# A 256-token, two-block network on one core: where the last weights, keys and first expert rows are loaded, and who turns retention's queries and keys

## The reference, cut to what matters

```python
def rotary(x, pos):
    cos, sin = jnp.cos(ang), jnp.sin(ang)
    x1, x2 = x[..., :half], x[..., half:]
    return jnp.concatenate([x1 * cos - x2 * sin, x1 * sin + x2 * cos], axis=-1)
# retention: q = rotary(q, pos); k = rotary(k, pos) * (RET_QK_DIM ** -0.5), 4 heads of 256

def one_block(xb):                                   # 256 tokens, 8 heads, 16 experts chosen per head
    qh = (xb @ wq).reshape(PEER_BLOCK, H_P, 2, D_QP // 2)
    s1 = jnp.einsum('thd,hnd->thn', qh[:, :, 0], sub_keys[0])
    s2 = jnp.einsum('thd,hnd->thn', qh[:, :, 1], sub_keys[1])
    v1, i1 = lax.top_k(s1, TOPK)
    v2, i2 = lax.top_k(s2, TOPK)
    cand = (v1[..., :, None] + v2[..., None, :]).reshape(PEER_BLOCK, H_P, TOPK * TOPK)
    sc, ci = lax.top_k(cand, TOPK)
    idx = ...                                        # i1 * 128 + i2 of the 16 best pairs
    gate_w = jax.nn.softmax(sc, axis=-1)
    act = jax.nn.gelu(jnp.einsum('thkd,td->thk', expert_u[idx], xb), approximate=False)
    return jnp.einsum('thk,thkd->td', gate_w * act, expert_v[idx])
```

## Time and profile before

| what | us |
|---|---|
| median of 3 runs | 1898.67 |
| lowest and highest | 1896.62, 1901.51 |
| the profiled execution, whole | 1897.0 |
| its span in the trace | 1895.7 |

### The profile page before, as it was taken

How to read it: one execution, slowest core, us unless ns; L and a number is a source line. 1 busy time by engine, 2 the same in 40 slices (tenths; PEclk the granted TensorE clock), 3 DMA queues, 4 the chain that set the end, 5 groups by cost and what they waited for, 6 DMA issues and landing times.

```text
span 1895.7 us, 23366 instructions
## 1 busy us (share of the span) xinstructions
PE 1712.7 (90%) x9248; PEld 1305.8 (69%) x9248; DVE 1201.8 (63%) x2123; ACT 748.2 (39%) x1314; POOL 414.2 (22%) x359
## 2 busy tenths in 40 slices
PE   7989999999999998989999999887888877787879
PEld 6869988977799888989989988873333333333333
DVE  5776654685566547864352665778667776667754
ACT  4555543434445435874353644442112212112211
POOL 0330000130000000003011000135454454454441
PEclk9999999999999999999999999999898898988889
DMA  6325555444455553422231323599999999999997
GB/s 246 111 102 185 194 180 196 164 158 169 149 178 187 181 189 140 164 108 91 88 112 47 110 89 125 183 422 378 422 421 421 422 421 421 422 420 422 421 422 295
DMA packets 62668, 453.87 MB, mean 239 GB/s; under 512 B 6968, under 2 KB 7096, under 8 KB 7904
## 3 DMA queue, kind: packets, MB, share of 16 engines
q0 software_dynamic: 36864, 268.45, 34.1%
q1 hardware_dynamic: 25040, 178.27, 26.2%
q10 hardware_dynamic: 656, 5.66, 0.8%
HBM read 451.15 MB, written 1.05 MB: 239 GB/s over the span
## 4 chain that ended last, share of the span: by engine, by line
PE 26%; DMA 17%; DVE 4%; ACT 2%; issue 1%; POOL 0%; DVEq 0%
DMA uv_rows<-expert_uv,index 16%; PE banks L2404 13%; PE banks L564 3%; PE banks L566 3%; PE banks L565 3%; DVE uv_rows L2551 2%; PE banks L2223 1%; PE banks L1894 0%; PE banks L1883 0%; POOL uv_rows L2574 0%; DMA sb_peer<-constants_peer 0%; DVE weights_lo L559 0%; PE banks L2370 0%; ACT diag L2455 0%; PE banks L1876 0%
## 5 line engine op out<-in xcount | busy, mean ns | idle before, releaser
L2404 PE MATMUL banks<-uv_rows,diag 128*128 128x512 f32 x1024 | 506.2, 658 | 123.3 <-ACT diag L2455 118.1
L559 DVE TENSOR_TENSOR weights_lo<-weights,weights_hi 128x1024 fp32r<-128x1024 f32 x336 | 419.0, 1288 | 262.5 <-ACT weights_hi L550 262.4
L2404 PEld LDWEIGHTS banks<-uv_rows,diag 128*128 128x128 f32 x1024 | 214.0, 212 | 414.9 <-issue 267.5
L550 ACT ACTIVATE weights_hi<-weights 128x1024 fp32r<-128x1024 f32 x336 | 336.9, 1052 | 373.9 <-PE banks L566 358.4
L564 PE MATMUL banks<-x_hi,weights_hi 128*128 128x256 f32 (+1 forms) x1472 | 428.6, 291 | 11.0 <-DVE weights_lo L559 5.5
L566 PE MATMUL banks<-x_hi,weights_lo 128*128 128x256 f32 (+1 forms) x1472 | 421.6, 286 | 0.0
L565 PE MATMUL banks<-x_lo,weights_hi 128*128 128x256 f32 (+1 forms) x1472 | 421.4, 286 | 0.0
L2551 DVE CUSTOM_DVE_ANT_0 uv_rows<-uv_rows,tokens 128x1024 f32<-128x1024 f32 x256 | 306.3, 1224 | 161.9 <-DMA uv_rows<-expert_uv,index 161.9
L2574 POOL DMA_INDIRECT uv_rows<-expert_uv,index x256 | 310.1, 1211 | 345.5 <-PE banks L2404 287.1
L564 PEld LDWEIGHTS banks<-x_hi,weights_hi 128*128 128x128 f32 x1472 | 283.3, 192 | 17.1 <-DVE weights_lo L559 7.4
L566 PEld LDWEIGHTS banks<-x_hi,weights_lo 128*128 128x128 f32 x1472 | 283.1, 192 | 0.0
(11 more groups left out here) (377 smaller groups left out, 2086.0 us busy)
## 6 DMA issues: line engine op xcount, KB each, us to landing
weights<-weights SPq DMA_DIRECT2D x168, 1024.0 KB, 4.8
uv_rows<-expert_uv,index POOLq DMA_INDIRECT x256, 18.4
sb_first<-constants_first ACTq DMA_DIRECT2D x1, 1920.0 KB, 8.8
sb_always<-constants_always ACTq DMA_DIRECT2D x1, 1627.5 KB, 7.0
sb_peer<-constants_peer ACTq DMA_DIRECT2D x1, 1544.0 KB, 8.0
h<-x SPq DMA_DIRECT2D x1, 1024.0 KB, 5.7
out<-h SPq DMA_DIRECT2D x4, 256.0 KB, 4.7
sb_now<-constants_now ACTq DMA_DIRECT2D x1, 216.0 KB, 4.7
```

Source lines behind the costliest of these rows:

```text
L550: self.act.activation(self.w_hi[b % SLOTS][:, f], self.raw[b % SLOTS][:, f], ACT.Copy).then_inc(self.hi_made, 1)
L559: self.dve.tensor_tensor(self.w_lo[b % SLOTS][:, f], self.raw[b % SLOTS][:, f], self.w_hi[b % SLOTS][:, f], ALU.subtract).then_inc(self.lo ...
L2404: mm = pe.matmul(self.bank(2 * t + half), self.diag[:, k, :], self.uv[n % NUV][:, f], start=(u < NT and k == 0), stop=(u >= UNITS - NT and ...
```

## The change

It has four parts.

1. **Blocks 164 to 167** (`AHEAD` = 4) are no longer loaded into the weight slots but into four of the early row buffers: 164 and 165 as soon as the mixer's last sum is made, 166 and 167 right behind block 163, all before block 164 is used. Gathers 5 and 6 now go to the weight slots, 7 to 10 to the four ahead buffers; each waits for the low part of blocks 162 to 167 in turn.
2. **The keys** are loaded by ACT at the first merge step instead of behind the mixer's last row product.
3. **Rows 0 to 3** (`FIRST_ROWS`) are dotted, gated and added between query blocks 6 and 7 instead of after all of them. The key scores use banks 0, 1, 2, 3, 0, 2, 3, 2 (`SCORE_BANK`), so that banks 0 and 1 are free. Gathers 13 to 16 take the buffers of rows 0 to 3, and only 17 to 19 wait for PE's reading of block 167. DVE computes the tokens one block earlier, the dots of rows 0 to 3 after block 4's split and those of rows 4 to 7 ahead of block 7, chooses unit 1 over blocks 5 and 6 instead of 4 to 6, and chooses unit 2 after the third group of unit 0 instead of the second.
4. **Retention**: DVE turns queries and keys, two heads at a time, in four calls of six instructions of 128 x 2 x 256. POOL turns nothing.

```diff
-        self.uv += [slots_of[j] for j in (0, 1, 2, 4, 3, 5)]
+        self.ahead = self.uv[EARLY - AHEAD:]
+        self.uv = self.uv[:EARLY - AHEAD] + slots_of[:SLOTS] + self.ahead + [slots_of[j] for j in (2, 4, 3, 5)]
...
     def sync_blocks(self):
-        w = self.ins["weights"]
-        for b in range(N_BLOCKS):
+        w, own = self.ins["weights"], N_BLOCKS - AHEAD
+        for b in range(own):
+            if b == own - 1:
+                self.sp.wait_ge(self.rows_done.sem, self.rows_done.at("mix_out", 4))
+                self.sync_ahead(own)
+                self.sync_ahead(own + 1)
             if b >= SLOTS:
                 self.sp.wait_ge(self.lo_made, PARTS * (b - SLOTS + 1))
             self.sp.dma_start(self.raw[b % SLOTS][:, :], w[b]).then_inc(self.block_full[b % SLOTS], 16)
+        self.sync_ahead(own + 2)
+        self.sync_ahead(own + 3)
...
-            if s >= 5:
-                self.vector_rotate(s - 5)
+            if s >= 4 and s < 7:
+                self.vector_rotate(*((0, 0), (0, 1), (1, 0))[s - 4])
...
-                self.vector_rotate(3)
+                self.vector_rotate(1, 1)
...
-        pool.wait_ge(self.turns_scaled, 2)
-        for hd in range(RET_H):
-            pool.wait_ge(*self.cols_freed("ret_qk", 4 + hd))
-            self.rotate(pool, self.g_step, hd, 8 + 2 * hd, self.ret_tmp[:, 2:4, :], self.ret_rot_k)
...
+            if s == 0:
+                act.dma_start(self.t_peer[:, :], self.ins["constants_peer"]).then_inc(self.peer_landed, 16)
...
+            if s == st.n - 2:
+                pe.wait_ge(self.scored, NT * 5)
+                for k in range(FIRST_ROWS):
+                    self.tensor_row(k)
...
+            if s == 3:
+                self.scalar_gate(0)
+            if s == 5:
+                self.scalar_group(0, 0, 0, FIRST_ROWS)
...
+            if s == 7:
+                self.vector_dots(0, FIRST_ROWS, 2 * FIRST_ROWS)
...
-            elif 4 <= s < 7:
-                self.vector_choose(1, self.CHOICE[s % 4])
-            if s == 3:
+            elif s == 4:
+                self.vector_dots(0, 0, FIRST_ROWS)
+            elif s == 5:
+                self.vector_coefs(0, 0, 0, FIRST_ROWS)
+                self.vector_choose(1, "halves")
+            elif s == 6:
+                self.vector_choose(1, "pairs")
+                self.vector_choose(1, "index")
+            if s == 2:
...
-                if g == int(u == 0) and u + NT < UNITS:
+                if g == 2 * int(u == 0) and u + NT < UNITS:
...
-                if n in (EARLY, EARLY + 1):
-                    pool.wait_ge(self.lo_made, PARTS * (N_BLOCKS - 1 + n - EARLY))
-                if n in (EARLY + 2, EARLY + 4):
-                    pool.wait_ge(self.blocks_read, N_BLOCKS - 1 + (n - EARLY) // 4)
-                if n >= NUV:
-                    pool.wait_ge(self.added, n - NUV + 1)
+                if EARLY - AHEAD <= n < EARLY + SLOTS:
+                    pool.wait_ge(self.lo_made, PARTS * (N_BLOCKS - AHEAD - SLOTS + n - (EARLY - AHEAD) + 1))
+                elif n in (EARLY + SLOTS, AGAIN + FIRST_ROWS):
+                    pool.wait_ge(self.blocks_read, N_BLOCKS - (n < AGAIN))
+                if ROW_PRIOR[n] is not None:
+                    pool.wait_ge(self.added, ROW_PRIOR[n] + 1)
```

More of the change, by code:

```diff
@@ L37 @@
 EARLY = 9
+AHEAD = 4
+FIRST_ROWS = 4
 UNITS = PEER_H * NT
@@ L212 @@
 TURN_BANKS = {"ret": 4}
+AGAIN = EARLY + SLOTS + 2
+ROW_BUFFER, ROW_TURN, ROW_PRIOR = [], [], []
+for _n in range(UNITS * TOPK):
+    if _n < AGAIN:
+        _at = _n
+    elif _n < AGAIN + FIRST_ROWS:
+        _at = _n - AGAIN
+    elif _n < NUV + FIRST_ROWS:
+        _at = _n - FIRST_ROWS
+    else:
+        _at = ROW_BUFFER[_n - NUV]
+    _before = [m for m in range(_n) if ROW_BUFFER[m] == _at]
+    ROW_BUFFER.append(_at)
+    ROW_TURN.append(len(_before) + 1)
+    ROW_PRIOR.append(_before[-1] if _before else None)
+SCORE_BANK = (0, 1, 2, 3, 0, 2, 3, 2)
 class Program:
```

149 lines of the change are left out of this document (84 added, 65 removed).

## The result

The changed kernel took 1887.88 us by the median of 5 runs (1884.95 to 1889.90), the kernel before 1898.67: a ratio of 0.9944, with a 95% interval of 0.9932 to 0.9956. The prediction was 1887.3. The profiled execution took 1885.42, its span 1884.0 where it was 1895.7: 11.7 us less, predicted 11.4.

The account below looks back on a forecast made before the run. PE's products were taken to set the time ahead of the experts, DMA gathers of expert rows the last third. 7.5 + 2.4 + 4.7 - 4.5 + 1.3 = 11.4 us off 1898.67 gave 1887.3 us, range 1880.5 to 1894.0.

Parts of the forecast that it names:

- Bound and model: Expert gathers: DMA full at 421 GB/s from 3.4 us behind gather 0's issue; 4.7 us lost dry at gather 24.
- Part 2: Keys loaded early: PE's 2.55 us wait for them goes, gather 0 comes 2.4 us earlier (2.0 to 2.7).
- beside nothing but each other: Weight blocks 165 to 167, loaded ahead of gather 0, were to share the DMA with no other load.
- Part 3: Rows between query blocks: old 4.7 us gap goes, new gaps of 2.3 and 2.2 us at gathers 10 and 20.
- price of a restart: DMA refill after a gap: 3.4 us from issue to full rate; with about 2.0 us, gaps total 3.1 instead of 4.5.
- Part 1: Weights ahead: blocks 165 to 167 leave the gather stage, 3 x 2.49 = 7.5 us gained.
- Part 4: Retention: PE's wait for a low part at 393.90 us goes, 1.3 us gained, lower bound -2.
- Never dry: Rival, expert gathers: the DMA never runs dry; gain 16.2 us, time 1882.5 us; chance 0.14.
- Short ring: Rival, expert gathers: gaps at 10 and 20 double, another 2 us at 24 or 32; time 1893.8 us; chance 0.12.
- Doesn't do what it says: Rival: first choice waits as long for something else, retention gives nothing; gain 7.7 us, time 1891.0 us; chance 0.10.
- Clock over blocks 3 to 6: Rival: PE stays at the 1.2 GHz level through query blocks 3 to 6, 5.7 us more each; 1907 us; chance 0.04.

Follow-up runs that it names:

- changed_again: The changed kernel measured once more, unaltered, beside other kernels on the same chip: 1890.42 us, 0.9960 of the kernel before.
- old_order: The changed kernel with rows 0 to 3 added after all query blocks again, with the old banks, groups, dots and choices: 1897.71 us, 0.9991 of the kernel before.
- blocks_in_slots: The changed kernel with AHEAD = 0, all weight blocks loaded through the two slots as before: 1891.51 us, 0.9970 of the kernel before.
- blocks_late: The changed kernel with weight blocks 166 and 167 loaded only once the first choice is made, behind gather 0: 1890.60 us, 0.9964 of the kernel before.
- rows_behind: The changed kernel with PE adding rows 0 to 3 behind query block 7 and the buffer order undone; dots, Gelu, choices kept: 1893.31 us, 0.9972 of before.
- pool_turns: The changed kernel with the retention's turns as before, queries on DVE, keys on POOL, one head at a time: 1889.01 us, 0.9955 of the kernel before.
- early_group: The changed kernel with rows 4 to 7's coefficients and diagonals ahead of the last scores, third choice behind four rows of unit 1: 1889.69 us, 0.9957 of before.
- evict_first: The changed kernel with ACT, behind retention's last query/key block, copying the bank out before splitting the next weight block: 1883.86 us, 0.9921 of the kernel before.

## Why the prediction was right, and where it was not

**The total** was right to 0.6 us, and the steps on which it rests were mostly right one by one. That it was right to 0.6 is luck in part: the second measurement, at 0.9960, gives 3.2 us less, and the executions scatter by more than that. Stage by stage, the prediction had 7.7 us for the gathers and 8.4 came, 2.4 for the keys and 2.3 came, 1.3 for the retention and 1.8 came, of which the profiled execution lost 0.8 again to the clock.

- *Bound and model*: right. What the DMA carries and how long it idles was all that changed behind gather 0 (7.5 + 4.7 - 3.8 = 8.4 us, as measured), and 3.4 us from issue to full rate described the start of the changed kernel too (346 GB/s in the window from 1225 is a DMA full from 1225.9).
- *Part 2*: 2.4 predicted, 2.29 measured. That the early load costs nothing held too: from PE's wait of 1.43 us (just ahead of the load) to the mixer's last product, changed_again takes 48.6 us, as the kernel before. What the prediction did not see is that the old place would have cost 6.7 us beside part 1; "beside nothing but each other" was true of the weights only because the keys had gone. Undone alone, part 2 takes back the whole gain.
- *Part 3*: gather 10 was predicted at 1250.4 and came at 1249.7, gather 20 at 1277.5 and came at 1275.8; the gaps were 2.3 + 2.2 = 4.5 predicted, 2.0 + 1.8 = 3.8 measured. With the measured issues the model gives (1249.72 - 1222.26) - 24.9 = 2.6 and (1275.79 - 1249.72) - 24.9 = 1.2, together 3.7, less than 4.5 because gather 20 came 53.5 us behind gather 0 and not 54.3 (gather 0 itself came at 1222.26, predicted 1223.2). These two differences also show a slip of mine: the time from issue to full rate stands at both ends of each stretch and cancels. The prediction said that the price of a restart weighs here, and that with the 2 us of the Trainium skill (page DMA: Bandwidth & Descriptors, section Anatomy of one DMA) the gaps would be 3.1; with any price that is the same at each start they are what the issues make them, and these windows can't tell 3.4 from 2. PE's granted clock behind its idle time ahead of gather 20 was 0.50 again, as in the earlier trace rows. Gather 32 came at 1305.8 (predicted 1306) and is as late as gather 20: it had nothing to spare.
- *Part 1*: the 7.5 us are a wrong price, though the sum with them is right. The sum holds for all parts together, since it takes the DMA's busy and idle time of one order as a whole. It may not be read part by part: alone the blocks are worth 1.5 (old_order against before), last they are worth 4.8 (blocks_in_slots against changed).
- *Part 4*: 1.3 predicted, 1.8 measured between the two profiles, which both kept the clock, and about nothing in an execution in which PE's clock falls behind the wait at 387. The turns came at 0.68 (predicted 0.69). The wait of 1.29 us went; where the other 0.5 came from is open. The step that failed is the clock: the prediction took the 1.00 of its one trace for granted.
- *Never dry*: false, the two dips are there. *Short ring*: false, nothing at 24 or 32 but the refill. *Doesn't do what it says*: false. *Clock over blocks 3 to 6*: false; behind the 2.15 us the clock was 0.66 in the window 1225 to 1230 and 1.00 from 1230 to 1260.

## What to carry to other kernels

Where a ring of buffers feeds a saturated DMA, write for each transfer "issue time + what is still to come at full rate" and look for the largest: that one sets the end, freeing bandwidth ahead of it is worth little until it moves (1.5 of 7.5 us here), and the next largest says what the move can bring at most. A sum of gains is good for the whole change and says nothing on a part; undo the parts one at a time before crediting them, since here one of them (the keys) was worth three times its price once another had filled the DMA beside it. And read the waits that a change leaves alone: copying a bank out before the next split, in another stage, took another 4 us off the median, 1.9 of them whatever the clock did.

## What the hardware showed

- The same wait is not always followed by the same clock. Behind PE's idle 2.86 us at 387 the granted clock was 1.00 in the profiles of before, changed, blocks_late, blocks_in_slots and rows_behind and fell to the 1.2 GHz level (0.50 in windows of 5 us right behind it) in six others; behind the idle 2.15 us at gather 0 it fell in most and stayed at 1.00 in pool_turns and early_group. The fall costs 2.8 us in the first place, 1.5 in the second. With the first wait cut to 0.9 us, neither of two profiles shows the fall. Whether that holds in every execution is not shown, and a short wait is no safeguard: behind PE's idle 0.51 us in the mixer (near 1027), with PE busy and the clock at 1.00 ahead of it, the clock was 0.50 in the profiles of before, changed_again and evict_first and 0.66 in that of the changed kernel.
- POOL's issue of a gather took 0.94 us alone, and 1.68 to 2.09 where it began inside a DVE instruction that reads two large tiles. Gather 20 was issued at 1275.79, just behind the start of a dot (1275.74 to 1276.96), and its issue ended at 1277.77; gather 1, issued at 1224.65 as DVE's split began at 1224.66, took 0.94. The Trainium skill, page SBUF — State Buffer, section SBUF: two separate sides, has DVE and GpSimd lock a shared port against each other for whole instructions, whoever starts first; these rows agree with it. Whether it cost time here is not shown: most issues found the DMA with work queued, but gather 0, at 2.09 us, found it idle.
